# Sample attention with 32 array columns per batch element, keys and values moving, and alternating array halves in the fills of head pairs

## The reference, cut to what matters

```python
# sample attention in the mixer: 8 query heads on 4 kv heads, 256 cached tokens per element, all of them attended
s = einsum('bkgqd,bkgqmd->bkgqm', qg, k_sel) * scale     # against the cached keys
s_own = einsum('bkgqd,bkmd->bkgqm', qg, own_k) * scale   # against the 4 new tokens, causal
p = softmax(concatenate([s, s_own]))
out = p_own @ own_v + p_past @ v_sel
# cross-attention of the samples: 4 heads, own cached memory keys and values per element
s = einsum('bthd,bmhd->bhtm', q, mk) * XA_HEAD_DIM ** -0.5
o = einsum('bhtm,bmhd->bthd', softmax(s), mv)
```

## Time and profile before

| | |
|---|---|
| three runs | 958.0, 958.16, 955.32 us; median 958.0 |
| the profiled execution | 956.8 us, span 955.1, mean granted TensorE clock 0.955 |
| TensorE | 915.8 us busy (96%), 6566 passes |
| VectorE, ScalarE, POOL | 639.5 (67%), 455.0 (48%), 133.1 us (14%) |
| DMA | 137.68 MB, 144 GB/s over the span |

### The profile page before, as it was taken

The page is one execution under the profiler, slowest core; times in us unless marked ns, Lnnn a source line. Parts: engine busy times, 40 slices in busy tenths (PEclk is TensorE's granted clock), DMA queues, the critical chain, the costliest instruction groups (busy, mean ns, idle before and its releaser), DMA issues.

```text
span 955.1 us, 17339 instructions
## 1 busy us (share of the span) xinstructions
PE 915.8 (96%) x6566; PEld 861.7 (90%) x6566; DVE 639.5 (67%) x1296; ACT 455.0 (48%) x896; POOL 133.1 (14%) x237
## 2 busy tenths in 40 slices
PE   5889999998999999999989999999899999999996
PEld 4889988996789999999989989899768999999996
DVE  4567863673378999974455786456436899998543
ACT  4452541434457666653444254234344766665332
POOL 1412310242000000000241231005210000000001
PEclk9989998899689999999999999989978999999999
DMA  8654631196236556555556554108641665565432
GB/s 256 185 133 142 179 90 46 56 255 183 63 89 174 153 160 176 175 161 175 152 142 165 167 169 124 45 18 224 182 134 51 170 173 153 160 177 162 157 123 67
DMA packets 209405, 137.68 MB, mean 144 GB/s; under 512 B 23475, under 2 KB 202203, under 8 KB 209323
## 3 DMA queue, kind: packets, MB, share of 16 engines
q1 hardware_dynamic: 199904, 111.11, 41.3%
q0 software_dynamic: 8288, 22.85, 8.3%
q10 hardware_dynamic: 1131, 2.62, 0.8%
HBM read 131.11 MB, written 5.44 MB: 143 GB/s over the span
## 4 chain that ended last, share of the span: by engine, by line
PE 91%; DVE 3%; DMA 2%; ACT 2%; issue 1%; ACTq 0%; DVEq 0%; SPq 0%
PE banks L1206 21%; PE banks L1207 21%; PE banks L1208 21%; PE banks L1384 3%; PE banks L1466 2%; PE banks L1474 2%; PE banks L1349 2%; PE banks L1306 2%; PE banks L1201 2%; PE banks L1434 2%; PE banks L1300 1%; PE banks L1362 1%; DMA ring<-in_w_in 1%; PE banks L1316 1%; PE banks L1415 1%
## 5 line engine op out<-in xcount | busy, mean ns | idle before, releaser
L1208 PE MATMUL banks<-mix_r,ring_r 128*128 128x288 f32 x1008 | 300.2, 298 | 0.0
L1208 PEld LDWEIGHTS banks<-mix_r,ring_r 128*128 128x128 f32 x1008 | 193.5, 192 | 0.0
L1206 PE MATMUL banks<-mix_r,ring_r 128*128 128x288 f32 x480 | 151.1, 315 | 9.8 <-ACT keysT L921 3.7
L1207 PE MATMUL banks<-XG_r,keysT_r 128*128 128x288 f32 x384 | 113.3, 295 | 0.0
L1092 ACT CAST ring_r<-ring 128x1024 fp32r<-128x1024 f32 x60 | 62.4, 1046 | 101.8 <-DMA ring<-in_w_in 76.1
L1206 PEld LDWEIGHTS banks<-mix_r,ring_r 128*128 128x128 f32 x480 | 93.8, 196 | 16.5 <-issue 9.2
L1207 PE MATMUL banks<-XG_r,ring_r 128*128 128x288 f32 x352 | 107.2, 305 | 0.0
L1624 DVE TENSOR_TENSOR ring_r<-ring,keysT_r 128x2048 fp32r<-128x2048 f32 (+1 forms) x36 | 80.2, 2228 | 37.2 <-ACT keysT_r L1092 37.2
L1208 PE MATMUL banks<-phase_r,ring_r 128*128 128x288 f32 x352 | 103.4, 294 | 0.0
L1207 PE MATMUL banks<-XG_r,vals_r 128*128 128x288 f32 x320 | 94.4, 295 | 0.0
L1906 DVE SCALAR_TENSOR_TENSOR phase<-phase,fpar 128x304 f32<-128x304 f32 x176 | 86.1, 531 | 3.9 <-ACT phase L1136 0.6
(11 more groups left out here) (301 smaller groups left out, 2015.0 us busy)
## 6 DMA issues: line engine op xcount, KB each, us to landing
ring<-in_w_up SPq DMA_DIRECT2D x88, 512.0 KB, 5.2
ring<-in_w_in SPq DMA_DIRECT2D x36, 512.0 KB, 4.3
ring<-in_w_down SPq DMA_DIRECT2D x16, 1024.0 KB, 5.2
ring<-in_w_down SPq DMA_DIRECT2D x8, 768.0 KB, 4.8
rawk<-in_cache_k POOLq DMA_DIRECT2D x32, 128.0 KB, 2.8
vals<-in_cache_v POOLq DMA_DIRECT2D x32, 128.0 KB, 2.5
ring<-in_w_in SPq DMA_DIRECT2D x16, 256.0 KB, 4.1
rawk<-in_cache_mem_k POOLq DMA_DIRECT2D x16, 256.0 KB, 4.7
```

Of the source, the lines that this page charges most:

```text
L1206: mm(out_, hi_w, hi_x, start=start, stop=False)
L1207: mm(out_, hi_w, lo_x, start=False, stop=False)
L1208: return mm(out_, lo_w, hi_x, start=False, stop=stop)
```

## The change

Sample attention: elements go in two groups ("half") of four. For each, the element's 32 query columns (two head pairs, 16 each) are stationary in 32 of the array's 128 columns, the element's keys move (256 columns), and the result lands in 32 of the 128 PSUM partitions. "ss" becomes one fill for both head pairs, followed by "sown" for the new tokens. The probabilities are not normalised before the transposes: the reciprocal is applied as "so" is emptied. In "so" the 32 probability columns of an element are stationary and its values move; the result has queries in partitions, so ScalarE copies it to `gathered`, and a new fill "so_turned" transposes it back. "ys", "yt", "yo" and "yo_turned" do the same for the cross-attention. "so" now stands ahead of "hn".

Pairs: the products of half 0 and half 1 alternate in "as", "diag", "diag_s", "level", "cross" (TensorE waits for both banks first), "ao", "ho", "hstate" and "xov"; "level" runs its small sample tiles first.

```diff
-    a("D", "ss", 0)
+    a("D", "ss")
+    a("D", "sown")
...
-    a("op", "snorm", 0)
+    a("op", "snorm")
...
-    a("op", "sq", 1)
...
-    a("A", "st", 0)
+    a("A", "st")
+    a("A", "st_own")
     a("D", "ho", 0)
     a("D", "ho", 1)
-    a("D", "ss", 1)
-    a("op", "snorm", 1)
+    a("A", "so")
     a("D", "hn", 0)
     a("D", "hn", 1)
-    a("A", "so", 0)
-    a("A", "st", 1)
     a("A", "mv", 0)
+    a("A", "so_turned")
     for k in (6, 7, 4, 5, 0, 1):
         a("op", "split_mixed", k)
     a("A", "mv", 1)
     a("op", "round", "out", 0, l)
     a("op", "rest", "out", 0, l)
-    a("A", "so", 1)
     for k in (2, 3):
...
-    a("A", "yo", 0)
+    a("A", "yo")
     a("A", "xt", 2)
...
-    a("A", "yo", 1)
+    a("A", "yo_turned")
     a("A", "xov", 1)
...
+                            for half in (0, 1):
+                                at = 16 * half + 8 * p + 4 * i
+                                src = qT[rows_i, p, SEQ + 16 * half:SEQ + 16 * half + 16].rearrange("p (b s) -> p b s", b=4)
+                                last = g_.tensor_copy(qx[rows_i, p, 4 * half:4 * half + 4, at:at + 4], src)
...
+                elif step == "sown":
+                    act.wait_ge(s["s_max"], l + 1)
+                    for half in (0, 1):
+                        last = ac(probs[:, half], probs[:, half], ACT.Exp, bias=small[:, 50 + half:51 + half], scale=SCALE,
+                                  accum_out=small[:, 52 + half:53 + half])
+                    last.then_inc(s["s_exp"], 1)
...
+                    act.wait_ge(s["s_r"], l + 1)
+                    act.wait_ge(filled, fill_no(l, step))
+                    for half in (0, 1):
+                        last = ac(gathered[:, half], bank(l, step)[:, 256 * half:256 * half + 256], ACT.Identity,
+                                  scale=small[:, 54 + half:55 + half])
+                    last.then_inc(emptied["A"], 1)
+                elif step == "so_turned":
+                    act.wait_ge(filled, fill_no(l, step))
+                    for p in (0, 1):
+                        for i in (0, 1):
+                            rows_i = slice(64 * i, 64 * i + 64)
+                            src = bank(l, step)[rows_i, 256 * p:256 * p + 256].rearrange("p (b x) -> p b x", b=8)
+                            src = src[:, :, 16 * p + 8 * i:16 * p + 8 * i + 8].rearrange("p b (g s) -> p g b s", g=2)
+                            dst = qT[rows_i, 2 * p:2 * p + 2, SEQ:N].rearrange("p g (b s) -> p g b s", b=8)
+                            last = nc.scalar.copy(dst, src)
...
+                    act.wait_ge(s["y_r"], l + 1)
+                    act.wait_ge(filled, fill_no(l, step))
+                    ac(gathered, bank(l, step).rearrange("p (h n) -> p h n", h=2), ACT.Identity,
+                       scale=small[:, 79:80]).then_inc(emptied["A"], 1)
+                elif step == "yo_turned":
+                    act.wait_ge(filled, fill_no(l, step))
+                    for p in (0, 1):
+                        for i in (0, 1):
+                            rows_i = slice(64 * i, 64 * i + 64)
+                            for half in (0, 1):
+                                at = 16 * half + 8 * p + 4 * i
+                                src = bank(l, step)[rows_i, 256 * p + P * half:256 * p + P * half + P]
+                                src = src.rearrange("p (b x) -> p b x", b=4)[:, :, at:at + 4]
+                                dst = mix[rows_i, p, SEQ + 16 * half:SEQ + 16 * half + 16].rearrange("p (b s) -> p b s", b=4)
+                                last = nc.scalar.copy(dst, src)
...
+            PAIRED = ("diag", "diag_s", "level", "cross", "as")
...
+                if step in PAIRED and args[-1] == 1:
+                    continue
+                if step in PAIRED:
+                    pe.wait_ge(emptied[banks.before[fill - 7][0]], banks.before[fill - 7][1])
+                    pair = [ps[:, (fill + i) % 8, :] for i in (0, 1)]
+                    half = [slice(0, 64), slice(64, 128)]
...
+                        mm(o[r[i], 0:P], vn[:, 0, kv[i]], probT[:, i, 0:P], start=True, stop=True)
+                    for i in (0, 1):
+                        mm(o[r[i], P:SEQ], vn[:, 0, kv[i]], probT[:, i, P:SEQ], start=True, stop=False)
+                    for i in (0, 1):
+                        last = mm(o[r[i], P:SEQ], vn[:, 1, kv[i]], probT[:, i, SEQ:384], start=False, stop=True)
...
-                    for b in range(8):
-                        last = mm(o[:, 0:256], qs[:, P * b:P * b + P], keysT[:, p, b], start=b == 0, stop=b == 7)
+                    for half in (0, 1):
+                        for p in (0, 1):
+                            for b in range(4):
+                                last = mm(o[32 * b:32 * b + 32, 256 * half:256 * half + 256], qs[:, p, 4 * half + b],
+                                          keysT[:, p, 4 * half + b], start=p == 0, stop=p == 1, skip_group_check=True)
+                elif step == "sown":
+                    for half in (0, 1):
+                        for p in (0, 1):
+                            last = mm(o[:, NS * half:NS * half + NS], qs[:, p, 4 * half:4 * half + 4].rearrange("p b r -> p (b r)"), kT[:, p, SEQ:N],
+                                      start=p == 0, stop=p == 1, skip_group_check=True)
...
                 elif step == "so":
+                    wait_emptied(pe, l, "st_own")
                     pe.wait_ge(vals_in, 16 * (24 * l + 16))
+                    for half in (0, 1):
+                        cols = slice(256 * half, 256 * half + 256)
+                        mm(o[:, cols], ownT[:, P * half:P * half + P], vn[0:NS, 2], start=True, stop=False, skip_group_check=True)
                         for j in (0, 1):
+                            for b in range(4):
+                                c = P * j + 32 * b
+                                last = mm(o[32 * b:32 * b + 32, cols], probsT[:, half, c:c + 32], vals[:, 4 * half + b, j],
+                                          start=False, stop=j == 1, skip_group_check=True)
+                elif step == "so_turned":
+                    wait_emptied(pe, l, "so")
+                    for p in (0, 1):
+                        for half in (0, 1):
+                            c = P * (2 * p + half)
+                            last = tr(o[:, c:c + P], gathered[:, half, P * p:P * p + P], ident[:])
...
+                    tiles = (2, 0, 1) if m < DEC_SEQ else (0, 1)
+                    for t in tiles:
                         for p in (0, 1):
                             n, c = (P, slice(P * t, P * t + P)) if t < 2 else (NS, slice(SEQ, N))
                             at = 64 * (2 * t + p) if t < 2 else 256 + NS // 2 * p
+                            for o, r in zip(pair, half):
+                                q = hq[r, p, c].rearrange("p (n two m) -> p n two m", two=2, m=m)[:, :, 1]
+                                last = mm(o[0:n, at:at + n // 2], hk[r, p, c], q, start=True, stop=True)
+                                if (t, p) == (1, 1):
+                                    last.then_inc(filled, 1)
+                    continue
...
+                        mm(o[r[i], 0:P], vh[:, 0, c[i]], sc[:, i, p], start=True, stop=True)
+                    for i in (0, 1):
+                        mm(o[r[i], P:SEQ], vh[:, 0, c[i]], sc[:, i, 4 + p], start=True, stop=False)
+                    for i in (0, 1):
+                        mm(o[r[i], P:SEQ], vh[:, 1, c[i]], sc[:, i, 2 + p], start=False, stop=True)
+                    for b in range(8):
+                        at = slice(SEQ + 4 * b, SEQ + 4 * b + 4)
+                        for i in (0, 1):
+                            mm(o[r[i], at], s0[r[i], p, b], hq[r[i], p, at], start=b == 0, stop=False, skip_group_check=True)
+                    for i in (0, 1):
+                        last = mm(o[r[i], SEQ:N], vh[0:NS, 2, c[i]], scs[0:NS, i, p], start=False, stop=True, skip_group_check=True)
...
-                            last = mm(o[64 * p:64 * p + 64, 0:256], qs[:, 576 * p + 64 * b:576 * p + 64 * b + 64], keysT[:, p, b],
-                                      start=b == 0, stop=b == 7)
+                    for half in (0, 1):
+                        for p in (0, 1):
+                            for b in range(4):
+                                last = mm(o[32 * b:32 * b + 32, 0:256], qx[:, p, 4 * half + b], keysT[:, p, 4 * half + b],
+                                          start=(half, p) == (0, 0), stop=(half, p) == (1, 1), skip_group_check=True)
...
+                    wait_emptied(pe, l, "ys")
...
+                            for b in range(4):
+                                c = P * j + 32 * b
+                                last = mm(o[32 * b:32 * b + 32, 256 * half:256 * half + 256], probsT[:, 0, c:c + 32],
+                                          vals[:, 4 * half + b, j], start=j == 0, stop=j == 1, skip_group_check=True)
+                elif step == "yo_turned":
```

(53 more changed lines are left out.)

184 lines of the change are left out of this document (65 added, 119 removed).

## The result

The changed kernel takes 900.31 us (median of four runs, 898.47 to 905.15) against 957.21 for the kernel before; the ratio is 0.941, 95% interval 0.9372 to 0.9447. The prediction said 898 and 880 to 925. The profiled execution is the slowest of the four: span 903.5 us against 955.1, 51.6 less where the medians differ by 56.9.

The account below looks back on a forecast made before the run. TensorE, 91% of the chain that ended last, was taken to bound the kernel. Tail 26, cross-attention 22.4 and front 10 sum to 58.4 us off the profiled 956.8: forecast 898, range 880 to 925.

Parts of the forecast that it names:

- The strips: In the sample-attention fills: passes in four column strips stream all at once, so a fill of 32 passes takes 1.8 us.
- Rival (1): Fewer strips stream at once: two at once gives 912 us (chance 0.14), none 939 us (chance 0.05).
- (3): Rival: half clock all through the mixer's tail and the cross-attention; chance 0.04, its time not in the text given.
- The tail: End of the mixer, both layers: shorter fills less new waits save 26 us, after 2 given back for half clock.
- the term for "so": In the mixer's tail: "so" takes 2.75 us, per half one 32-row product (0.47) and 8 products in strips (0.9).
- the wait at "out" 0: In the mixer's tail: TensorE waits 4.5 us for the normalisation of "ho" on VectorE and ScalarE; ends 0 and 6.
- the wait at head pair 3: In the mixer's tail: "at" of that pair waits 0.4 us for a softmax the shortened scores no longer cover.
- The chain of 13.4: Normalisation work ahead of "out" 0, put at 13.4 us against 8.9 of TensorE work covering it.
- half clock around the new wait: In the mixer's tail: 2 us of the gain given back for TensorE at half speed near the "out" 0 wait.
- Cross-attention: Both layers: 13.5 and 12.9 us less, 2 per layer given back, 22.4 in all; ScalarE's queue sets "xo"'s start.
- no better than 0.78: Sign of a wrong prediction: mean clock in the cross-attention no better than 0.78 (0.88 in the mixer's tail).
- The front: Start of the mixer, both layers: pairing halves, mostly in "level", saves 10 us; ends 4 and 11.

## Why the prediction was right, point by point

**The strips.** Right: four passes start within 0.02 us, and the fill takes 1.86 at full clock (1.8 predicted). Rival (1) is out. So is the case to which (3) gives 0.04, half clock all through the tail and the cross-attention: their mean clocks are 0.91 and 0.85 in the first layer, 0.91 and 0.77 in the second. Rival (1)'s bounds were too wide: even a program that does one strip after another would have paid 4.5, not 7.0.

**The tail.** 21.2 us in place of 26, and the step that failed is the term for "so" and its clock. The other terms hold: "ss" 1.86 (1.8 predicted), "ho" twice 2.07 (2.1), the wait at "out" 0 3.9 and 4.5 (4.5); the wait at head pair 3 is 0.9 and 0.8 (0.4). (Some of the sums are loose. The added fills come to 10.45, not 10.6, and 17.8 - 4.9 + 0.4 is 13.3, not 13.5. The chain of 13.4 leaves out the two copies of 1.0 that it names; with them the wait would be 5.5, and 3.7 to 5.1 is what the kernels show that keep "out" 0 in its place, but for one wait of 3.0.) "so" was put at 2.75 and takes 3.25 at full clock (0.62 for each 32-row product and 1.0 for its strips, where the prediction had 0.47 and 0.9) and 5.6 and 5.9 in this execution, mostly at half clock, which sets in right behind "ho". The prediction had named few moving columns as what half clock falls on in "yo", and it took 2 us off for half clock around the new wait. It left out that "ho" keeps its 4-column passes and that "so" is what now stands behind them. In the kernel before, half clock fell on the second "ho" and the second "ss" (158.7 to 168.9). The runs with 32 columns in "ho", full clock in four layers of four, show the cause.

**The output projection** was no term, and lost 3.1. Part is half clock behind the wait at "out" 0 (171.9 to 175.3, and 602.0 to 605.4, where the kernel before had none); part is small waits at the transposes of the memory keys, 0.4 us in the first layer, where the trace names no releaser, and 1.2 in the second, 1.0 of it for their load. That POOL issues this load behind other work is shown to be the next limit once "out" 0 starts early; with POOL's order alone altered the small waits stayed.

**Cross-attention.** 21.0 in place of 22.4. "xo" was put at 25.3 us after the stretch's start (251.5 on the old clock) and starts at 25.7 in the first layer, behind ScalarE, as said (moving one weight rounding of 1.9 us out of its way brought it 1.4 forward), and takes 9.2 us for the 7.9 predicted, at half clock from 236.8 to 240.2. In the second layer the half clock of 17 us brings its start to 29.2. Put at "no better than 0.78" as a sign of failure, the mean clock of 0.77 there shows that this sign was badly chosen: the slow time fell from 2 x 0.22 x 46.1 = 20.3 us to 2 x 0.23 x 36.8 = 16.9, and the gain came from the fills.

**The front.** 13.3 against 10; the levels are at 1.27 and 1.04 (1.45 and 1.03 predicted), and some 1.7 of the rest is a half-clock stretch at 83.6 that isn't there after and came back when the pairs were undone. Undoing them costs 8.5 to 10.5.

The total by medians, 56.9 against 58.4, is nearer than its parts, and that is partly luck: "so" and the output projection lost some 9 us in this profile, the front gave 3 more, and other executions have less half clock.

## What to carry to other kernels

Products with few rows of output can be turned so that the small operand is stationary in a quarter of the array and the large one moves; four such strips, written in turn, cost what one costs here (32 passes start within 1.56 us, the eight of one strip alone within 1.54), and the order in which they are written decides it: 1.86 us a fill, or 4.52 one strip after the other, though waits behind the fills hid most of that here. When TensorE's work shrinks, look for what was hidden behind it, on every queue: here ScalarE's rounding and VectorE's remainder, both foreseen, and then a load that POOL issues behind other work, visible as a long wait, 5.5 us, only once the one for the remainder was gone. And weigh a reordering with the clock that follows it: at "out" 0 waits shorter by 7.6 us gave back 13, once the load behind them was early enough.

## What the runs showed of the hardware

TensorE took up passes for a free strip ahead of their turn, past the last three passes of each strip under way and not past more (0.89 us between the strips' starts, with passes 0.22 apart). "ho" with 4 moving columns was followed by half clock on what came next in 14 of 20 layers, and with "mk" 1 next in one of two, wide products and all (5.2 us for 3.46); with 32 columns in as many passes and the same time (2.09 against 2.07 us a fill) it was not, in four layers of four. And with a wait of 3.0 to 5.1 us ahead of "out" 0, 3.4 to 6.8 us at 0.5 set in during the wait or within 1.2 us of its end, in 15 of 16 layers (of two waits of 3.0, one had none); in the ten layers in which the wait was 1.4 and less there is none.

The granted clock is 1 or 0.5 in every profile of this case, with nothing between. The passes of "xo" in the kernel before show what that is for 288 columns: they start 0.48 us apart up to 267.6, at 0.5, and 0.24 apart from 268.0, at 1. A pass lasts over the next start: 0.41 us there for 0.24 between starts, and in "ss" one strip after the other 0.38 for 0.22; so durations added up say more time than goes by. A split product's three passes of 288 columns are 0.40 us from start to start (0.13 each, from 273.5 in the kernel before), the two passes of an unsplit one 0.49. With few columns moving, passes start 0.11 apart under 128 weight columns ("so" before, 32 passes in 3.48) and 0.06 apart under 64 ("ho" before, 16 passes in 1.02).
